# A decoder trunk on one core: gates, branch outputs and their gated sum laid out with tokens on partitions, the sum turned by TensorE

## What is computed

```
h = rmsnorm(x, norm_mix)
... y_a (sliding window attention), y_b (block attention), y_c (SSD scan) ...
gates = jax.nn.sigmoid((h @ w_gate + b_gate).astype(jnp.float32)).astype(x.dtype)
g_a, g_b, g_c = jnp.split(gates, N_BRANCH, axis=-1)
merged = g_a * (y_a @ w_br_swa) + g_b * (y_b @ w_br_moba) + g_c * (y_c @ w_br_ssd)
x = x + merged @ w_mix_out
```

## Time and profile before

| | us |
|---|---|
| median of 3 runs | 1179.04 |
| lowest, highest | 1178.24, 1179.38 |
| profiled execution | 1178.97 |
| its span, first to last instruction | 1177.2 |
| TensorE busy | 1166.1 |
| VectorE busy | 775.1 |
| ScalarE busy | 596.3 |
| POOL busy | 61.1 |

### The profile page before, as it was taken

How to read it: one execution, slowest core, us unless ns; L and a number is a source line. 1 busy time by engine, 2 the same in 40 slices (tenths; PEclk the granted TensorE clock), 3 DMA queues, 4 the chain that set the end, 5 groups by cost and what they waited for, 6 DMA issues and landing times.

```text
span 1177.2 us, 18388 instructions
## 1 busy us (share of the span) xinstructions
PE 1166.1 (99%) x7491; PEld 1036.0 (88%) x7491; DVE 775.1 (66%) x1199; ACT 596.3 (51%) x870; POOL 61.1 (5%) x93
## 2 busy tenths in 40 slices
PE   8999999999999999999999999999999999999997
PEld 7988899999998888888889888999989988888886
DVE  7876856987455475665578677579775455766565
ACT  5656564445454354444455666453555444544443
POOL 1000003300000000000000000033000000000000
PEclk9999999999999999999999999999999999999999
DMA  7744426765644456556456443455755443755660
GB/s 238 237 143 132 156 85 187 220 213 176 194 143 151 136 180 204 188 180 199 159 156 205 144 144 108 140 172 191 250 179 180 144 143 111 244 182 180 202 208 37
DMA packets 156428, 201.31 MB, mean 171 GB/s; under 512 B 7168, under 2 KB 111928, under 8 KB 156344
## 3 DMA queue, kind: packets, MB, share of 16 engines
q1 hardware_dynamic: 155616, 199.58, 53.2%
q10 hardware_dynamic: 728, 0.55, 0.1%
HBM read 199.04 MB, written 1.08 MB: 170 GB/s over the span
## 4 chain that ended last, share of the span: by engine, by line
PE 94%; DMA 2%; DVE 1%; issue 1%; ACT 1%; POOL 1%; SPq 0%; POOLq 0%; DVEq 0%; ACTq 0%
PE psum L1153 12%; PE psum L1154 12%; PE psum L1155 12%; PE psum L1164 11%; PE psum L1165 10%; PE psum L1139 10%; PE psum L1167 10%; PE psum L1140 5%; PE psum L1186 1%; PE psum L1318 1%; PE psum L1356 1%; DMA raw<-in_w_gate_dram 1%; PE psum L1329 1%; PE psum L1374 1%; PE psum L1397 1%
## 5 line engine op out<-in xcount | busy, mean ns | idle before, releaser
L1499 DVE TENSOR_TENSOR w_lo<-raw,w_hi 128x2048 fp32r<-128x2048 f32 (+1 forms) x182 | 408.9, 2251 | 221.3 <-ACT w_hi L755 220.7
L755 ACT ACTIVATE w_hi<-raw 128x2048 fp32r<-128x2048 f32 (+1 forms) x182 | 341.6, 1879 | 158.2 <-PE psum L1167 109.6
L1153 PE MATMUL psum<-act_both,w_hi 128*128 128x256 f32 x832 | 241.0, 290 | 0.0
L1154 PE MATMUL psum<-act_both,w_hi 128*128 128x256 f32 x832 | 235.2, 283 | 0.0
L1155 PE MATMUL psum<-act_both,w_lo 128*128 128x256 f32 x832 | 235.2, 283 | 0.0
L1139 PE MATMUL psum<-act_both,w_hi 128*128 128x512 f32 x512 | 182.1, 400 | 0.0
L1153 PEld LDWEIGHTS psum<-act_both,w_hi 128*128 128x128 f32 x832 | 159.2, 191 | 4.1 <-issue 3.0
L1154 PEld LDWEIGHTS psum<-act_both,w_hi 128*128 128x128 f32 x832 | 159.3, 192 | 0.6 <-issue 0.5
L1155 PEld LDWEIGHTS psum<-act_both,w_lo 128*128 128x128 f32 x832 | 159.2, 191 | 0.0
L1140 PE MATMUL psum<-act_both,w_lo 128*128 128x256 f32 x512 | 143.7, 281 | 0.0
L1139 PEld LDWEIGHTS psum<-act_both,w_hi 128*128 128x128 f32 x512 | 96.2, 188 | 24.6 <-DVE act_both L1528 0.7
(11 more groups left out here) (261 smaller groups left out, 1928.2 us busy)
## 6 DMA issues: line engine op xcount, KB each, us to landing
raw<-in_w_in_dram SPq DMA_DIRECT2D x34, 1024.0 KB, 5.2
raw<-in_w_up_dram SPq DMA_DIRECT2D x32, 1024.0 KB, 5.4
raw<-in_w_down_dram SPq DMA_DIRECT2D x32, 1024.0 KB, 5.0
raw<-in_w_gate_dram SPq DMA_DIRECT2D x24, 1024.0 KB, 7.3
raw<-in_w_ckv_dram SPq DMA_DIRECT2D x16, 1024.0 KB, 5.3
raw<-in_w_br_ssd_dram SPq DMA_DIRECT2D x8, 1024.0 KB, 5.4
raw<-in_w_mix_out_dram SPq DMA_DIRECT2D x8, 1024.0 KB, 5.0
raw<-in_w_cq_dram SPq DMA_DIRECT2D x8, 1024.0 KB, 5.2
```

The source lines that it names most:

```text
L755: act.activation(w_hi[:, slot, 0:n], raw[:, slot, 0:n], ACT.Copy).then_inc(hi_ready.sem, 1)
L1153: pe.matmul(dst, m_hi[:, k, cs], a_hi[:, k, :], start=k == 0, stop=False)
L1154: pe.matmul(dst, m_hi[:, k, cs], a_lo[:, k, :], start=False, stop=False)
L1499: dve.tensor_tensor(w_lo[:, slot, 0:n], raw[:, slot, 0:n], w_hi[:, slot, 0:n].bitcast(F32), ALU.subtract).then_inc(lo_ready.sem, 1)
```

## The change

The gate and branch units (21 to 40) go to orientation B, so that gates, branch outputs and their sum have tokens on partitions. The number of units, their order and their weights stay as they are. What follows from it:

- The bias is now a row along the free axis. It is loaded to all 128 partitions by three DMAs of 512 KB in each layer on SyncE's queue (ahead of the weights of units 12, 30 and 34) and added by an instruction of its own. For gates a and b, VectorE adds it while it reads the bank; ScalarE's tanh then waits for VectorE. For gate c, ScalarE copies the bank out, POOL adds the bias, and ScalarE makes the tanh (`last_gate`, after `hi(u+3)`).
- Gates are read after a stripe, in slots 22, 24, 28, 30, 34 and 36. The two banks of a stripe must both be free before its first matmul.
- The sum has to be turned for unit 41: 8 transposes after unit 39 and 8 within unit 41 (`merged_turn`). ScalarE and VectorE split it from the banks. The turning of the memory's norm moves from slot 41 to slot 42.
- Branch c no longer waits for closing 6 at its start, but at tile 1 of unit 37, and for closing 7 at tile 1 of unit 38.

```
-    stripes_a("gate", "w_gate", 0, "h", 4)
+    stripes_b("gate", "w_gate", 0, "h", 2)
     for j in range(2):
-        unit("branch_a", "A", "w_br_swa", 0, 4, 512 * j, 512, "y_swa", j)
+        stripe_b("branch_a", "w_br_swa", 512 * j, 512, "y_swa", j, (4,))
...
-NORM_TURN_SLOT = {1: U_MIX, 2: U_QX - 2}
+NORM_TURN_SLOT = {1: U_MIX + 1, 2: U_QX - 2}
+MERGED_TURN_SLOT = (U_BRC + 2, U_MIX)
...
+                    for i, (slot, bias) in enumerate(((U_VB, bias_ab), (U_BRB - 1, bias_ab), (U_BRB + 3, bias_c))):
+                        if u == slot:
...
+                            sp.dma_start(bias[:], a["b_gate"][l, D * i:D * (i + 1)].partition_broadcast(P))\
+                              .then_inc(bias_loaded.sem, 16)
...
+                pool.wait_ge(*bias_loaded.at(l, 16 * 3))
+                for j in range(2):
+                    for t in range(TT):
+                        g, cs = g_sb[:, t, 512 * j:512 * (j + 1)], slice(512 * j, 512 * (j + 1))
+                        pool.wait_ge(*is_read(l, unit_bank(U_BRC - 4 + 2 * j, t)))
+                        pool.tensor_tensor(g, g, bias_c[:, cs], ALU.add).then_inc(gate_biased.sem, 1)
...
+                if kind == "gate":
+                    if u > U_BRB:
+                        act.wait_ge(*is_read(l, unit_bank(U_BRB + 1, 1)))
+                        act.wait_ge(*unit_done.at(l, u + 1))
+                        for t in range(TT):
+                            out_of_bank(l, unit_bank(u, t), g_sb[:, t, 512 * j:512 * (j + 1)])
+                        return
+                    for t in range(TT):
+                        g = g_sb[:, t, 512 * j:512 * (j + 1)]
+                        act.wait_ge(*is_read(l, unit_bank(u, t)))
+                        act.activation(g, g, ACT.Tanh, scale=0.5).then_inc(gate_made.sem, 1)
+                    return
...
-                    for m in range(2):
-                        b0 = PC_BGATE + branch * KT + tile + m
-                        ins = act.activation(g_sb[:, tile + m, :], bank((u, 0))[:, m * SEQ:(m + 1) * SEQ],
-                                             ACT.Tanh, bias=half[:, l, b0:b0 + 1], scale=0.5)
-                    ins.then_inc(free((u, 0)), 1)
+
+            def last_gate(l, j):
+                for t in range(TT):
+                    g = g_sb[:, t, 512 * j:512 * (j + 1)]
+                    act.wait_ge(*gate_biased.at(l, 2 * j + t + 1))
+                    act.activation(g, g, ACT.Tanh, scale=0.5).then_inc(gate_made.sem, 1)
...
+            def merged_turn(l, j):
+
+                for t in range(TT):
+                    key = ("mergedT", j, t)
+                    pe.wait_ge(*mg_ready.at(l, 2 * j + t + 1))
+                    pe.wait_ge(*is_free(l, key))
+                    for k in range(4):
+                        c = 512 * j + k * P
+                        ins = pe.transpose(bank(key)[:, k * P:(k + 1) * P], mg_sb[:, t, c:c + P], ident[:])
+                    ins.then_inc(full(key), 1)
...
+                elif kind == "gate":
+                    if u > U_BRB:
+                        return
+                    branch, cs = w["col"] // D, slice(512 * j, 512 * (j + 1))
+                    dve.wait_ge(*bias_loaded.at(l, 16 * (branch + 1)))
+                    for t in range(TT):
+                        key = unit_bank(u, t)
+                        dve.tensor_tensor(g_sb[:, t, cs], bank(key), bias_ab[:, cs],
+                                          ALU.add).then_inc(free(key), 1)
```

More of the change, by code:

```diff
@@ L248, in slot_banks @@
             out.append((YB_, ("closeT", i)))
+    if s in MERGED_TURN_SLOT:
+        out += [((TB_, OB_)[t], ("mergedT", MERGED_TURN_SLOT.index(s), t)) for t in range(TT)]
     for n in (1, 2):
@@ L737, in trunk @@
         NCONST = 16
-        NPAR = 16 * 7
+        NPAR = 16 * 6
         @block.scalar
@@ L1015, in _ @@
                         norm_gain_hi(l, 3, ((0, 1), (2, 3))[u - U_CO - 2])
+                    for j in range(2):
+                        if u == MERGED_TURN_SLOT[j] + 1 - j:
+                            merged_hi(l, j)
                     evacuate(l, u)
@@ L1024, in _ @@
                         sines()
+                    if w["kind"] == "gate" and w["last"] and u > U_BRB:
+                        last_gate(l, w["index"])
                     if w["kind"] == "up":
@@ L1159, in unit @@
                             inner(l, u)
+                        if t == 1 and u in (U_BRC, U_BRC + 1):
+                            pe.wait_ge(*is_read(l, ("closeT", 6 + u - U_BRC)))
+                        if w["act"] == "merged":
+                            part = w["row"] // 512
+                            pe.wait_ge(*mg_hi.at(l, 2 * part + t + 1))
+                            if part == 0:
+                                pe.wait_ge(*is_read(l, ("mergedT", 0, t)))
                         dst = bank(unit_bank(u, t))[:, 0:n]
@@ L1713, in evacuate @@
                     return
-                if not w["last"] or kind in ("qkb", "vb", "kx", "qx", "gate", "down"):
+                if not w["last"] or kind in ("qkb", "vb", "kx", "qx", "down"):
                     return
@@ L1755, in evacuate @@
                                                  ALU.add, ALU.mult).then_inc(free(key), 1)
-                elif kind in ("branch_a", "branch_b", "branch_c"):
-                    for i, key in enumerate(unit_banks(u, w)):
-                        c = w["col"] // P + 2 * i
-                        g, mg = g_sb[:, c:c + 2, :], mg_sb[:, c:c + 2, :]
-                        if i == 0:
-                            wait_read(dve, l, [(v, 0) for v in range(u - 8, u) if UNITS[v]["kind"] == "gate"])
+                elif kind == "gate":
+                    if u > U_BRB:
+                        return
+                    branch, cs = w["col"] // D, slice(512 * j, 512 * (j + 1))
+                    dve.wait_ge(*bias_loaded.at(l, 16 * (branch + 1)))
+                    for t in range(TT):
+                        key = unit_bank(u, t)
+                        dve.tensor_tensor(g_sb[:, t, cs], bank(key), bias_ab[:, cs],
+                                          ALU.add).then_inc(free(key), 1)
+                elif kind in ("branch_a", "branch_b", "branch_c"):
+                    branch = ("branch_a", "branch_b", "branch_c").index(kind)
+                    for t in range(TT):
+                        key, cs = unit_bank(u, t), slice(512 * j, 512 * (j + 1))
+                        g, mg = g_sb[:, t, cs], mg_sb[:, t, cs]
+                        dve.wait_ge(*gate_made.at(l, 4 * branch + 2 * j + t + 1))
+                        if (u, t) == (U_BRC + 3, 1):
+                            dve.wait_ge(*unit_done.at(l, u + 1))
                         if kind == "branch_a":
-                            dve.scalar_tensor_tensor(mg, g, 1.0, two(bank(key)), ALU.add, ALU.mult)\
+                            dve.scalar_tensor_tensor(mg, g, 1.0, bank(key), ALU.add, ALU.mult)\
                                .then_inc(free(key), 1)
                             continue
-                        part = two(tmp[:, i, :])
-                        dve.scalar_tensor_tensor(part, g, 1.0, two(bank(key)), ALU.add, ALU.mult)\
+                        part = tmp[:, t, :]
+                        dve.scalar_tensor_tensor(part, g, 1.0, bank(key), ALU.add, ALU.mult)\
                            .then_inc(free(key), 1)
@@ L1792, in merged_lo @@
             def merged_lo(l, j):
-                dve.wait_ge(*mg_hi.at(l, j + 1))
-                cs = slice(2 * j, 2 * j + 2)
-                dve.scalar_tensor_tensor(act_lo[:, cs, :], mg_sb[:, cs, :], 0.5, act_hi[:, cs, :].bitcast(F32),
-                                         ALU.mult, ALU.subtract).then_inc(mg_lo.sem, 1)
+                for t in range(TT):
+                    key, ks, ts = ("mergedT", j, t), slice(4 * j, 4 * j + 4), slice(t * P, (t + 1) * P)
+                    dve.wait_ge(*mg_hi.at(l, 2 * j + t + 1))
+                    dve.scalar_tensor_tensor(act_lo[:, ks, ts], bank(key).rearrange("p (k n) -> p k n", n=P), 0.5,
+                                             act_hi[:, ks, ts].bitcast(F32), ALU.mult, ALU.subtract)\
+                       .then_inc(free(key), 1)
             def relu_low(l, j):
@@ L1943, in _ @@
                             close_lo_part(l, i)
+                    for j in range(2):
+                        if u == MERGED_TURN_SLOT[j] + 1 - j:
+                            merged_lo(l, j)
                     if 0 <= job_at(u):
```

71 lines of the change are left out of this document (37 added, 34 removed).

## The result

| | before | after |
|---|---|---|
| median, us | 1179.10 | 1191.82 (1191.12 to 1193.29) |
| profiled span, us | 1177.2 | 1190.4 |
| TensorE / VectorE busy, us | 1166.1 / 775.1 | 1166.0 / 790.0 |
| ratio after / before | | 1.0112, 95% interval 1.0097 to 1.0127 |

The account below looks back on a forecast made before the run. TensorE bound the kernel, with VectorE nearly equal in slots 30 to 34. Per layer 4.9 - 1.3 + 1.9 + 0.3 = 5.8 us, in two layers 11.6, gave 1190.6 us; 8 in 10 range 1180.5 to 1198.

Parts of the forecast that it names:

- the prediction's three terms: From unit 37 on, us per layer: clean units 37 to 40 -1.3, transposes +1.9, second transpose set's wait for VectorE +0.3.
- rate and transposes alone: Per layer, orientation B saves 4.3 us on TensorE and 16 more transposes cost 1.9; alone these give 1174.2 us.
- The chain through VectorE: Slots 28 to 34: additions delay the tanh, then high and low parts; TensorE starts unit 35 4.7 us late per layer.
- unit 35 started with its low part ready: Sign against the forecast: the additions would then be hidden and the time that of the first two rivals.
- The entry to the chain: Slot 28, layer 0: closing ends at 205.9 instead of 206.29, and unit 31's low part comes 2.5 us later.
- slots 22 and 24 cost nothing in the end: A turn of job 15 waits about 1.5 us; low parts with 5 to 10 us in hand absorb it before slot 28.
- TensorE's waits: TensorE waits for VectorE about 2 us before closing 5's turn, 1 before unit 32, 2.4 before unit 33.
- The granted clock: TensorE's granted clock stays at full speed despite the waits.
- POOL: Slots 34 to 36: POOL's gate c additions slow VectorE's low part of unit 37 by 0 to 2.1 us; unit 37 taken 4.9 late.
- The rival in which ScalarE's high parts of units 38 and 40 delay TensorE: POOL's additions take 2.9 us each; unit 40 or the turned sum another 3 us late per layer: 1196.6 us, 14%.
- Only the additions lie on the path: Unit 33's high part is ready as before, so the delay is 1.4 us, not 5.7: 1183.0 us, 14%.
- The queues follow: VectorE and ScalarE take the additions into their pauses; rate and transposes alone decide: 1174.2 us, 8%.

Follow-up runs that it names:

- the last experiment: Changed kernel with high parts before the tanh, gate c's additions late, sums and bias additions in VectorE's pauses, gate c's bias loaded ahead of unit 37's weights: 1173.86 us.
- High parts first: Changed kernel, but in slots 22, 24, 28 and 30 ScalarE makes the high part of unit u+3 before the gate's tanh: 1181.16 us, ratio 1.0019.
- Sums behind the low parts: High parts first with gate c's additions late, and branch b's sums moved behind the low parts of units 34 and 35: 1178.81 us, ratio 1.0004.

## Why the prediction was right, and where it was not

- **TensorE's rate and the transposes.** In clean stretches of the changed kernel matmuls are 0.227 us apart, and each set of 8 transposes takes 0.79. From unit 37 to unit 41 it saved nothing (23.05 against 23.04 us, the first transposes included), from 41 to 45 it lost 1.0; together +1.0, where the prediction's three terms give +0.9. The 1174.2 of rate and transposes alone was reached, by the last experiment (1173.86, 4.6 below the kernel before on its chip; forecast 4.8). By the gap of 2.5 ns that the Trainium skill gives for one matmul by itself ("TensorE: Matmul & The Clock Gate", "Back-to-back issue gap") 20 units would save 1.2 per layer and the floor would be 1180.3; eight kernels here with all units in orientation B lie below that, three of them without a part of the biases. The measurements decide for the rows. For a stream of weight loads and matmuls the same section gives about 131 ns at 512 columns, and the 227 here doesn't fit that either.
- **The chain through VectorE.** Its links have the forecast sizes: closing 5, additions, tanh, high part, low part in the forecast order, the low part 6.0 us behind the end of the closing (224.17 to 230.15; forecast 6.2). *High parts first* shows that this order was the cause of most of it. Step by step the kernels give 1176.14 without any bias, 2.3 more with gate c's (1178.44), 2.7 more with the additions on VectorE (1181.16), and 10.7 more with the tanh ahead of the high parts (1191.82).
- **How it reached TensorE.** This part of the mechanism was half right. The waits ahead of the turn of closing 5 and of units 32 and 33 came, but the prediction also lets TensorE wait for the low part of unit 35, and names "unit 35 started with its low part ready" as a sign against itself. The low part was ready at 250.23, 0.1 us before the start, and TensorE did not wait there; it had waited for closing 5's `y_tok` and for banks that VectorE had yet to read (units 32 and 33, the values ahead of unit 34). The additions were not hidden all the same, since these and the low part hang on the same queue. *Sums behind the low parts* shows the difference: an earlier low part alone brought nothing.
- **The entry to the chain was off in layer 0.** Closing 4 ended at 207.36, forecast 205.9, and the low parts of units 31 to 33 follow 1.3 to 2.2 later than forecast: unit 35 at 250.35, forecast 248.8. The step that failed is "slots 22 and 24 cost nothing in the end". There too the tanh stands ahead of the high parts: with high parts first unit 24 starts at 166.76 instead of 167.70, the high part of unit 30 at 195.44 instead of 197.53, and closing 4's scaling at 204.78 instead of 206.87. Of these 2.1 us the order explains 0.9, by which the weights of unit 30 were asked for later (189.13 against 188.21); the rest is that they took 8.4 us to come instead of 7.2. In layer 1 of the changed kernel they took 6.2, and closing 4 ended about as forecast there: at 793.65, which is 205.3 in layer 0's terms (unit 22 starts 588.3 us later). Why that load varies is open. In layer 1 unit 35 was 4.0 late, less than the forecast 4.7. The two errors nearly cancel (7.7 and 5.5, forecast 5.8 each); that the sum came out at 1190.6 against 1191.82 is partly luck.
- **TensorE's waits.** Forecast 2, 1 and 2.4 us ahead of the turn of closing 5, of unit 32 and of unit 33; measured 1.73, 0.63 and 1.08. Ahead of the last the clock had already cost some 1.6 us. Missing from the list was the 1.00 for POOL ahead of the values after unit 30. It cost nothing further, since VectorE's waits come behind it.
- **The granted clock** was forecast at full speed. It was not (below). It didn't matter for the time of this kernel, as VectorE's queue was later still. The version without gate c's bias bears that out: in its layer 1 the clock was low for 6.8 us instead of 3.4, TensorE waited 0.17 and 0.33 us ahead of units 32 and 33 instead of 0.63 and 1.07, and unit 35 came 225.2 us after the layer's first unit in both.
- **POOL.** Forecast 0 to 2.1, taken 0.6 of the 1.2 on unit 37 over unit 35; measured 0.95 per layer with gate c's bias left out. It agrees with the shared interface that the Trainium skill names ("GPSIMD Engine Reference", "Key points"). The rival in which ScalarE's high parts of units 38 and 40 delay TensorE did not come: the tanh waited (259.17, 260.59), the high part of unit 38 came at 261.13, and its low part still had 3.0 us in hand.
- **The rivals.** "Only the additions lie on the path", 1183.0, is what the kernel does with the high parts first (1181.16). "The queues follow", 1174.2, is what it does when the additions stand in pauses and the load is out of the way.

## What to carry to other kernels

A step that makes one engine wait for another costs what is queued behind the wait, not its own length: here two tanh of 0.63 us held back high parts of 1.92 us, and with them the whole pipeline. Put such a step behind the work that is needed next, and new work into a pause that the engine has anyway. When the order is mended, look for what each engine releases besides the obvious product (a bank of PSUM, a slot of the load queue): those were the next two bounds.
